# The end of the first expert mixture: three jobs spread by TensorE instead of two, and fetched rows added there

## The chip, the cores and the metric

The kernel runs on one core of a Trainium2 chip. The metric is device time in microseconds, taken as the median of three runs; before the change it is 1932.65 us (1932.41 to 1936.66). All data are 32-bit floats.

## The reference, cut to what matters

The program is two transformer blocks on 256 tokens of width 1024. The change lies in the mixture of experts at the end of the first block: 16 experts of hidden width 256, of which each token takes two.

```python
def hier_moe(h, lp):
    t = h.reshape(B * L, D)                        # 256 x 1024
    ...                                            # group, two experts per token, weights
    combine = jnp.sum(one_hot(e_idx, 16) * w_sel[..., None], axis=1)
    hg = jnp.einsum("nd,edh->neh", t, lp["moe_w_gate"])
    hu = jnp.einsum("nd,edh->neh", t, lp["moe_w_up"])
    a = silu(hg) * hu * combine[..., None]
    return jnp.einsum("neh,ehd->nd", a, lp["moe_w_down"])
...
x = x + mod_l[5] * hier_moe(modulate(rmsnorm(x, norm2_w[l]), mod_l[3], mod_l[4]), lp)
x = rmsnorm(x, norm_f_w)                           # and then the second block
```

## The kernel before, in words

The code calls this mixture `moe1`. It computes each expert only for the tokens that chose it. The 16 experts are taken two at a time, so there are eight **jobs**, numbered 0 to 7. A job has 128 places: 64 for its first expert, 64 for its second.

A job goes through these stages. TensorE gathers its tokens and turns them (`gather`); VectorE and ScalarE each copy one half of that to SBUF (`he_in`). TensorE multiplies by gate and up weights in four parts of one weight cell each (`pair_gate_up`, L1278). ScalarE takes the silu (L1924), VectorE multiplies (L2819) and transposes (L2822), and the semaphore `moe1_actT` tells TensorE. TensorE multiplies by the down weights in two cells (`pair_down`, L1289). VectorE and ScalarE copy the result into a buffer of rows, `pair_ye` (L2829 and L1931), 8 small copies each.

The loop over `s` in `pairs` sets the order on each engine. TensorE does gate and up of job s, with the gather of job s+1 behind the third cell, and then the down product of job s-1; behind the loop the last thing is the down product of job 7. So the down products of jobs 6 and 7 stand in a row.

The rows must get back to the tokens. Jobs 0 to 5 do this through HBM: ScalarE's queue stores the 128 rows of a job (L1937, 0.5 MB), and GpSimd fetches for each token the two rows of its two experts with four indirect DMAs (L679, 0.5 MB each), once these six stores have landed. VectorE weighs the fetched rows (`rows_in`, L2876 and L2879), and adds them to `x` with the block's gate (`add_gated`, L2588 and L2590, once per block of 128 tokens). Jobs 6 and 7 are spread instead: TensorE multiplies their rows by a matrix of weighted ones, `selT2` (the products of L1356: 4 of 128x512 for each job, two per block of tokens), and VectorE adds the sum with `add_gated` too. `SPREAD` says how many jobs are spread. Behind the spread TensorE runs 26 fill products (`busy`, L693), whose results nobody reads.

SyncE issues the loads of the weights into nine cells of 1 MB, in the order in which they are used; a cell is loaded again when TensorE has released it (semaphore `units_used`). The order of everything here is that of the code: no scheduler changes it.

Of the kernel before, what the change touches and what calls it, by code (L numbers as in the profile page):

```python
# [14 lines left out]
P = 128  # L15
T = 256
# [229 lines left out]
SPREAD = {"moe1": 2, "moe2": 1}  # L246
# [104 lines left out]
R_SELT, R_SELW, R_YE2, R_HOT = 512, 2560, 5120, 14464  # L351
# [29 lines left out]
def build(nc, A, blob_in, out):  # L381
    with ExitStack() as ctx:
# [236 lines left out]
        def _(pool):  # L619
# [29 lines left out]
            for i, name in enumerate(("moe1", "moe2")):  # L649
# [4 lines left out]
                with pool.Else():  # L654
# [32 lines left out]
        def _(pe):  # L687
# [545 lines left out]
            def moe_mm(name, i):  # L1233
# [9 lines left out]
                selw, selT2 = region(R_SELW, 2, NT, P), region(R_SELT, 2, T)  # L1243
                pair_actT, pair_ye = region(R_MT, 2, 4, 64), (region(R_YE, D), region(R_YE2, D))
# [63 lines left out]
                def gather(j, x0):  # L1308
# [12 lines left out]
                    if j == jobs - 1 and name == "moe2":  # L1321
                        for b in range(NT):
                            last = nc.tensor.transpose(ps[0:slot_n, x0 + 2, b * P:(b + 1) * P], sel[:, b, :], ident)
                    elif j == jobs - 1:
                        for i_ in range(2):
                            for b in range(NT):
                                last = nc.tensor.transpose(ps[:, j % 2, i_ * T + b * P:i_ * T + (b + 1) * P], selw[:, i_, b, :], ident)
                    last.then_inc(sem(f"{name}_gathered"), 1)

                def pairs():  # L1330

                    gather(0, 2)
# [18 lines left out]
                    for i_ in range(2):  # L1351
                        pe.wait_ge(sem("moe1_ye"), jobs - 1 + i_)
                        pe.wait_ge(sem("moe1_ye_dve"), jobs - 1 + i_)
                        for p in range(4):
                            b, half = divmod(p, 2)
                            last = mm(ps[:, p, :], selT2[:, i_, b * P:(b + 1) * P], pair_ye[i_][:, half * 512:(half + 1) * 512],  # L1356
                                      start=i_ == 0, stop=i_ == 1)
                            if i_:
                                last.then_inc(sem("moe1_spread"), 1)
                    busy(26, 4)  # L1360
# [350 lines left out]
        def _(act):  # L1711
# [184 lines left out]
            def moe_silu(name, i):  # L1896
# [7 lines left out]
                pair_sg, pair_ye = region(R_MG, 4, 64), (region(R_YE, D), region(R_YE2, D))  # L1904
# [9 lines left out]
                def pairs():  # L1914

                    he_in(0, 2)
                    for s in range(jobs + 1):
# [7 lines left out]
                        if s:  # L1925
                            j = s - 1
                            act.wait_ge(used, dn[j][-1][3])
                            if j >= 2:
                                act.wait_ge(sem(f"moe1_stored_{j % 2}"), 16 * (j // 2))
                            for t_, q in ((t_, q) for t_ in range(4) for q in (2, 3)):  # L1930
                                last = ac(pair_ye[j % 2][32 * t_:32 * t_ + 32, q * 256:(q + 1) * 256],  # L1931
                                          ps[32 * q:32 * q + 32, 4 + 2 * (j % 2) + t_ // 2, (t_ % 2) * 256:(t_ % 2 + 1) * 256], ACT.Copy)
                            last.then_inc(sem("moe1_ye"), 1)
                            if j < jobs - SPREAD[name]:
                                act.wait_ge(sem("moe1_ye"), j + 1)
                                act.wait_ge(sem("moe1_ye_dve"), j + 1)
                                act.dma_start(rows_of[name][j * slot_n:(j + 1) * slot_n, :], pair_ye[j % 2]).then_inc(sem(f"moe1_stored_{j % 2}"), 16)  # L1937
# [199 lines left out]
        def _(dve):  # L2137
# [562 lines left out]
            def moe_act(name, i, between):  # L2700
# [14 lines left out]
                selw, selT2 = region(R_SELW, 2, NT, 2, 64), region(R_SELT, 2 * T)  # L2715
# [4 lines left out]
                pair_sg, pair_act, pair_actT, pair_ye = region(R_MG, 4, 64), region(R_MA, 4, 64), region(R_MT, 2, T), (ye, region(R_YE2, D))  # L2720
# [9 lines left out]
                def select_weighted():  # L2730
                    for j in range(2):
                        for b in range(NT):
                            for e in range(2):
                                c = 2 * (jobs - 2 + j) + e
# [8 lines left out]
                def he_in(j, x0):  # L2743
# [5 lines left out]
                    if j == jobs - 1:  # L2749
                        if name == "moe1":  # L2750
                            v.tensor_copy(selT2, ps[:, j % 2, :])
                        else:
                            v.tensor_copy(selT, ps[0:slot_n, x0 + 2, 0:T])
# [55 lines left out]
                def pairs():  # L2809
# [4 lines left out]
                    for s in range(jobs + 1):  # L2814
                        if s < jobs:
                            if s + 1 < jobs:
                                he_in(s + 1, 2)
                            dve.wait_ge(sem("moe1_silu"), s + 1)
# [4 lines left out]
                        if s:  # L2823
                            j = s - 1
                            dve.wait_ge(used, down_[j][-1][3])
                            if j >= 2:
                                dve.wait_ge(sem(f"moe1_stored_{j % 2}"), 16 * (j // 2))
                            for t_, q in ((t_, q) for t_ in range(4) for q in (0, 1)):
                                last = v.tensor_copy(pair_ye[j % 2][32 * t_:32 * t_ + 32, q * 256:(q + 1) * 256],  # L2829
                                                     ps[32 * q:32 * q + 32, 4 + 2 * (j % 2) + t_ // 2, (t_ % 2) * 256:(t_ % 2 + 1) * 256])  # L2830
# [41 lines left out]
                def rows_in():  # L2872

                    dve.wait_ge(sem(f"{name}_rows"), 16 * NT * 2)
# [5 lines left out]
                    fence()  # L2880
                    for b in range(NT):
                        add_gated(b, 0, D, ya[:, b, :], 1)
# [356 lines left out]
```

## Time and profile before

| | |
|---|---|
| time, median of three runs | 1932.65 us |
| profiled execution, its own time | 1931.84 us |
| its span in the trace | 1930.0 us |
| mean granted TensorE clock | 0.991 |
| TensorE (PE) busy | 1832.1 us, 95% |
| VectorE (DVE) busy | 686.6 us, 36% |
| ScalarE (ACT) busy | 312.8 us, 16% |
| first mixture, from its first gate product to the last spread product | 505.6 to 643.7 us |

A time in a row is counted from the start of the span. A 32-bit matmul stands as two rows in the trace, each with a weight load (PEld) of its own; a transposition stands as one. Idle time ahead of an instruction stands in brackets with what ended it; "issue" means that nothing the profile shows was waited for. PEclk is the granted TensorE clock as a share of 2.4 GHz, so 0.50 is 1.2 GHz.

### The profile page before, as it was taken

The numbers are of one execution on the slowest core, as the hardware profiler recorded it, in microseconds if no ns is written. First come the engines' busy times: TensorE is split into PE (matmuls) and PEld (weight loads), VectorE is DVE, ScalarE is ACT, GpSimd is POOL, SyncE is SP. The second block draws the span as 40 slices with busy tenths as digits, with TensorE's granted clock in tenths as the row PEclk, the third lists the DMA queues.
The fourth block names the chain that finished last, engine by engine and source line by source line (L and its number), as shares of the span: only waits on it lengthen the run. The fifth ranks groups of instructions, "written<-read, shape, count | busy, mean of one in ns | idle before, by whom it ended". The sixth has DMA issues, their size and how long they took to land.

```text
span 1930.0 us, 38840 instructions
## 1 busy us (share of the span) xinstructions
PE 1832.1 (95%) x17312; PEld 1069.2 (55%) x17312; DVE 686.6 (36%) x1656; ACT 312.8 (16%) x729; POOL 35.3 (2%) x54
## 2 busy tenths in 40 slices
PE   5999989999887899999999999999999999999997
PEld 2655767885766555577676555443444444343443
DVE  3757782532333665432323553211110111111014
ACT  3221121001233324200001242100000010000001
POOL 0100000000100000000000000000000000000000
PEclk9999999999999999999999999999999999999999
DMA  9968743274799442467675332799999999999995
GB/s 356 370 221 305 262 172 115 85 264 163 281 405 419 162 160 103 151 236 256 229 250 181 131 101 112 288 399 420 409 420 410 415 411 406 419 413 415 408 416 214
DMA packets 157471, 547.75 MB, mean 284 GB/s; under 512 B 10224, under 2 KB 35152, under 8 KB 123072
## 3 DMA queue, kind: packets, MB, share of 16 engines
q1 hardware_dynamic: 149360, 509.15, 68.3%
q0 software_dynamic: 5152, 26.49, 3.9%
q10 hardware_dynamic: 2784, 9.53, 1.3%
q8 instruction: 140, 2.29, 0.5%
q14 instruction: 35, 0.29, 0.0%
HBM read 533.99 MB, written 18.48 MB: 286 GB/s over the span
## 4 chain that ended last, share of the span: by engine, by line
PE 86%; DVE 6%; DMA 2%; issue 2%; DVEq 1%; ACT 1%; SPq 0%; ACTq 0%
PE ps L1266 24%; PE ps L1302 12%; PE ps L1215 8%; PE ps L1499 8%; PE ps L1079 4%; PE ps L1197 4%; PE ps L1227 4%; PE ps L882 4%; PE ps L1278 3%; PE ps L1094 2%; PE ps L1289 1%; DMA ring<-in_ada_w 1%; PE ps L749 1%; PE ps L698 1%; PE ps L1549 1%
## 5 line engine op out<-in xcount | busy, mean ns | idle before, releaser
L1266 PE MATMUL ps<-ring,arena 128*32 128x512 f32 (+1 forms) x4608 | 459.1, 557 | 0.0
L1266 PEld LDWEIGHTS ps<-ring,arena 128*32 128x32 f32 x4608 | 148.9, 110 | 293.9 <-issue 289.5
L1302 PE MATMUL ps<-ring,arena 128*32 128x256 f32 x4224 | 232.1, 379 | 0.0
L1302 PEld LDWEIGHTS ps<-ring,arena 128*32 128x32 f32 x4224 | 137.3, 110 | 98.7 <-issue 12.1
L2851 DVE TENSOR_TENSOR arena<-arena,ps 128x256 f32<-128x256 f32 (+1 forms) x72 | 26.9, 373 | 390.9 <-ACT arena L1952 390.9
L1499 PE MATMUL ps<-ring,hT 128*128 128x512 f32 (+1 forms) x384 | 154.9, 554 | 1.4 <-DVE hT L2201 1.4
L1215 PE MATMUL ps<-hT,ring 128*128 128x256 f32 x704 | 153.8, 379 | 0.7 <-DVE hT L2201 0.7
L1215 PEld LDWEIGHTS ps<-hT,ring 128*128 128x128 f32 x704 | 133.6, 190 | 23.4 <-issue 4.8
L1499 PEld LDWEIGHTS ps<-ring,hT 128*128 128x128 f32 x384 | 69.1, 190 | 68.8 <-issue 66.9
L1079 PE MATMUL ps<-hT,ring 128*128 128x256 f32 x384 | 86.6, 385 | 3.9 <-DMA ring<-in_w_branch 3.9
L1952 ACT ACTIVATE arena<-ps 128x256 f32<-128x256 f32 (+1 forms) x72 | 21.2, 367 | 422.7 <-PE ps L1266 422.7
L1278 PE MATMUL ps<-ring,arena 128*32 128x128 f32 x2048 | 67.2, 285 | 22.8 <-issue 22.5
L882 PE MATMUL ps<-hT,ring 128*128 128x256 f32 x384 | 88.1, 383 | 0.8 <-DVE hT L2201 0.8
L2747 DVE TENSOR_SCALAR arena<-ps,ga,mod 128x128 f32<-128x128 f32 (+1 forms) x64 | 20.8, 388 | 188.8 <-PE ps L1317 140.9
L1079 PEld LDWEIGHTS ps<-hT,ring 128*128 128x128 f32 x384 | 73.8, 193 | 14.5 <-DMA ring<-in_w_branch 4.3
L882 PEld LDWEIGHTS ps<-hT,ring 128*128 128x128 f32 x384 | 71.4, 190 | 17.5 <-issue 6.6
L1227 PE MATMUL ps<-ring,arena 128*128 128x512 f32 x176 | 78.4, 596 | 0.0
L1278 PEld LDWEIGHTS ps<-ring,arena 128*32 128x32 f32 x2048 | 60.2, 115 | 28.8 <-issue 26.7
L2171 DVE SCALAR_TENSOR_TENSOR arena<-ring,cact,arena 128x512 f32<-128x512 f32 x84 | 63.1, 751 | 6.6 <-issue 0.4
L2279 DVE SCALAR_TENSOR_TENSOR grow<-arena,colv,grow 128x189 f32<-128x189 f32 (+2 forms) x160 | 62.1, 429 | 6.3 <-issue 0.4
L2697 DVE TENSOR_TENSOR arena<-arena,ps 128x256 f32<-128x256 f32 x22 | 9.3, 422 | 146.9 <-ACT arena L1894 146.9
L1910 ACT ACTIVATE arena<-ps,mod,ga 128x128 f32<-128x128 f32 (+1 forms) x64 | 23.2, 443 | 218.9 <-PE ps L1317 155.4
(426 smaller groups left out, 1784.9 us busy)
## 6 DMA issues: line engine op xcount, KB each, us to landing
ring<-in_gate_up SPq DMA_DIRECT2D x160, 1024.0 KB, 14.1
ring<-in_down SPq DMA_DIRECT2D x104, 1024.0 KB, 15.5
ring<-in_gate_up_last SPq DMA_DIRECT2D x64, 768.0 KB, 13.4
ring<-in_w_ada SPq DMA_DIRECT2D x48, 768.0 KB, 6.1
ring<-in_w_in SPq DMA_DIRECT2D x36, 768.0 KB, 7.3
ring<-in_ada_w SPq DMA_DIRECT2D x24, 768.0 KB, 10.4
ring<-in_w_ada SPq DMA_DIRECT2D x24, 512.0 KB, 7.1
ring<-in_w_in SPq DMA_DIRECT2D x12, 1024.0 KB, 7.5
```

Source lines behind the costliest of these rows:

```text
L882: last = mm(ps[:, half, (i % 2) * T:(i % 2 + 1) * T], quads[:, s, k * 512 + i * P:k * 512 + (i + 1) * P], src[:, k, :], start=k == 0, stop ...
L1079: last = mm(ps[:, 2 * (n % 2), i * T:(i + 1) * T], w512(s, k, m * P, P), hT[:, k, :], start=k == 0, stop=k == KD - 1)
L1094: last = mm(ps[:, 2 * (n % 2) + 1, i * T:(i + 1) * T], ring[:, s, o:o + P], z[:, y0 + c, :], start=c == 0, stop=c == NBR - 1)
L1197: last = mm(ps[:, 2 * b + half, :], src[:, k, b * P:(b + 1) * P], w512(slots_[half], k), start=k == 0, stop=k == KD - 1)
L1215: m_ = mm(ps[:, hb, i * cols:(i + 1) * cols], ring[:, s, o:o + P], src[:, k, :], start=k == 0, stop=k == KD - 1)
L1227: m_ = mm(ps[:, base + 2 * b + half, :], region(R_AT, 2, T)[:, hb, b * P:(b + 1) * P], ring[:, s, o:o + 512], start=first and hb == 0, sto ...
L1266: last = mm(ps[32 * q:32 * q + 32, base + t_, 0:2 * n], src[:, k, 32 * t_:32 * t_ + 32], w[:, q], start=k == 0, stop=k == KD - 1)
L1278: last = mm(ps[32 * q:32 * q + 32, bank, t_ * P:(t_ + 1) * P], src[:, k, 32 * t_:32 * t_ + 32], w[:, t_ // 2, q], start=k == 0 and t_ == 0 ...
L1302: last = mm(ps[32 * q:32 * q + 32, bank + t_ // 2, (t_ % 2) * 256:(t_ % 2 + 1) * 256], rows[:, t_, o:o + 32], cells[:, cell, r * D + q * 2 ...
L1499: last = mm(ps[:, b, 0:w], hT[:, k, b * P:(b + 1) * P], w512(entry[0], k, 0, w, w), start=k == 0, stop=k == KD - 1)
L2171: last = v.scalar_tensor_tensor(acc, w, cact[:, c + k:c + k + 1], acc, ALU.mult, ALU.add)
L2279: v.scalar_tensor_tensor(acc[:, a, ro, co], grids[a][:, ri, ci], tap(b, (dr + 1) * 3 + dc + 1), acc[:, a, ro, co], ALU.mult, ALU.add)
```

## The change

Job 5 is spread by TensorE too, so that five jobs and not six are stored and fetched. Three of job 5's four spread products stand inside the gate and up products of job 7, behind the third cell (`g == 2`). The rest stands behind the last down product. The weighted rows that were fetched are added in the same sums, by a product with the identity for each of the four banks, and VectorE then adds each block once. The weighing itself (`weigh_rows`) moves on VectorE from behind the last copies to the place ahead of job 7's silu product. The rows of job 7 get a third buffer. The selection matrix of job 5 is made and turned in addition. The fills go from 26 to 18.

```diff
-SPREAD = {"moe1": 2, "moe2": 1}
+SPREAD = {"moe1": 3, "moe2": 1}
+YE_OF = (0, 1, 0, 1, 0, 1, 0, 2)
...
                         for i_ in range(2):
-                            pool.wait_ge(sem(f"moe1_stored_{i_}"), 16 * (stored // 2))
+                            pool.wait_ge(sem(f"moe1_stored_{i_}"), 16 * ((stored + 1 - i_) // 2))
...
-                    elif j == jobs - 1:
-                        for i_ in range(2):
+                    elif name == "moe1" and j >= jobs - 2:
+                        for n, i_ in enumerate((0,) if j == jobs - 2 else (1, 2)):
                             for b in range(NT):
-                                last = nc.tensor.transpose(ps[:, j % 2, i_ * T + b * P:i_ * T + (b + 1) * P], selw[:, i_, b, :], ident)
+                                last = nc.tensor.transpose(ps[:, j % 2, n * T + b * P:n * T + (b + 1) * P], selw[:, i_, b, :], ident)
...
+                TO_BANK = (2, 3, 0, 1)
+                def copied(j):
+                    pe.wait_ge(sem("moe1_ye"), j + 1)
+                    pe.wait_ge(sem("moe1_ye_dve"), j + 1)
+                def spread_job(j, parts):
+                    i_ = j - (jobs - 3)
+                    for p in parts:
+                        b, half = divmod(p, 2)
+                        last = mm(ps[:, TO_BANK[p], :], selT2[:, i_, b * P:(b + 1) * P], pair_ye[YE_OF[j]][:, half * 512:(half + 1) * 512],
+                                  start=i_ == 0, stop=i_ == 2)
+                        if i_ == 2:
+                            last.then_inc(sem("moe1_spread"), 1)
...
                                 pair_gate_up(g, gu[s][g], he[:, s % 2], s % 2)
+                                if g == 2 and s == jobs - 1:
+                                    pe.wait_ge(sem("moe1_actT"), s)
+                                    copied(jobs - 3)
+                                    spread_job(jobs - 3, (0, 1, 2))
...
-                    for i_ in range(2):
-                        pe.wait_ge(sem("moe1_ye"), jobs - 1 + i_)
-                        pe.wait_ge(sem("moe1_ye_dve"), jobs - 1 + i_)
-                        for p in range(4):
-                            ...
-                    busy(26, 4)
+                    copied(jobs - 2)
+                    spread_job(jobs - 2, (0, 1, 2))
+                    spread_job(jobs - 3, (3,))
+                    spread_job(jobs - 2, (3,))
+                    for p in range(4):
+                        b, half = divmod(p, 2)
+                        mm(ps[:, TO_BANK[p], :], ident, rows_sum[:, b, half * 512:(half + 1) * 512], start=False, stop=False)
+                    copied(jobs - 1)
+                    spread_job(jobs - 1, range(4))
+                    busy(18, 4)
...
-                            if j >= 2:
+                            if 2 <= j < jobs - 1:
                                 act.wait_ge(sem(f"moe1_stored_{j % 2}"), 16 * (j // 2))
...
                 def select_weighted():
-                    for j in range(2):
+                    for j in range(3):
...
                             if s + 1 < jobs:
                                 he_in(s + 1, 2)
+                            if s == jobs - 1:
+                                weigh_rows()
                             dve.wait_ge(sem("moe1_silu"), s + 1)
...
-                    rows_in()
                     for b in range(NT):
                         dve.wait_ge(sem("moe1_spread"), 2 * b + 2)
-                        add_gated(b, 0, D, all_ps[:, b * D:(b + 1) * D], 1).then_inc(sem("block_in"), 1)
+                        add_gated(b, 0, D, all_ps[:, (1 - b) * D:(2 - b) * D], 1).then_inc(sem("block_in"), 1)
```

The new lines have other numbers: L1278 becomes L1280, L1289 becomes L1291, L1356 becomes L1344, L2876 becomes L2908, L2588 becomes L2611. On TensorE, from the third gate and up cell of job 7 on, there stood:

```order
L1278 MATMUL ps<-ring,arena 32x128 [waits cell3_full]
L1278 MATMUL ps<-ring,arena 32x128 x31
L1278 MATMUL ps<-ring,arena 32x128 [waits cell4_full]
L1278 MATMUL ps<-ring,arena 32x128 x31
...
L1289 MATMUL ps<-ring,arena 32x256 x15
L1356 MATMUL ps<-arena 128x512 [waits moe1_ye_dve,moe1_ye]
L1356 MATMUL ps<-arena 128x512 x3
L1356 MATMUL ps<-arena 128x512 [waits moe1_ye_dve,moe1_ye]
L1356 MATMUL ps<-arena 128x512 x3
L693 MATMUL ps<-blob 128x256 x26
```

and now there stands:

```order
L1280 MATMUL ps<-ring,arena 32x128 [waits cell3_full]
L1280 MATMUL ps<-ring,arena 32x128 x31
L1344 MATMUL ps<-arena 128x512 [waits moe1_ye_dve,moe1_ye,moe1_actT]
L1344 MATMUL ps<-arena 128x512 x2
L1280 MATMUL ps<-ring,arena 32x128 [waits cell4_full]
L1280 MATMUL ps<-ring,arena 32x128 x31
...
L1291 MATMUL ps<-ring,arena 32x256 x15
L1344 MATMUL ps<-arena 128x512 [waits moe1_ye_dve,moe1_ye]
L1344 MATMUL ps<-arena 128x512 x4
L1380 MATMUL ps<-arena,blob 128x512 x4
L1344 MATMUL ps<-arena 128x512 [waits moe1_ye_dve,moe1_ye]
L1344 MATMUL ps<-arena 128x512 x3
L694 MATMUL ps<-blob 128x256 x18
```

Three spread products are now ahead of the fourth cell, five and four identity products (L1380) ahead of the four of job 7. On VectorE, from the copies of job 5 on, there stood:

```order
L2829 COPY arena<-ps 32x256 x7
L2819 TENSOR_TENSOR arena<-arena,ps 128x256 [waits moe1_silu]
L2822 STREAM_TRANSPOSE arena<-arena 128x256
L2829 COPY arena<-ps 32x256 [waits moe1_stored_0,units_used]
L2829 COPY arena<-ps 32x256 x7
L2829 COPY arena<-ps 32x256 [waits moe1_stored_1,units_used]
L2829 COPY arena<-ps 32x256 x7
L2876 TENSOR_SCALAR arena<-arena 128x1024 [waits moe1_rows]
L2876 TENSOR_SCALAR arena<-arena 128x1024
L2879 SCALAR_TENSOR_TENSOR arena<-arena 128x1024 x2
L2588 TENSOR_TENSOR xn<-arena,grow 128x1024
L2590 TENSOR_TENSOR x<-x,xn 128x1024
```

and now there stands:

```order
L2855 COPY arena<-ps 32x256 x7
L2908 TENSOR_SCALAR arena<-arena 128x1024 [waits moe1_rows]
L2908 TENSOR_SCALAR arena<-arena 128x1024
L2911 SCALAR_TENSOR_TENSOR arena<-arena 128x1024 x2
L2845 TENSOR_TENSOR arena<-arena,ps 128x256 [waits moe1_silu]
L2848 STREAM_TRANSPOSE arena<-arena 128x256
L2855 COPY arena<-ps 32x256 [waits moe1_stored_0,units_used]
L2855 COPY arena<-ps 32x256 x7
L2855 COPY arena<-ps 32x256 [waits units_used]
L2855 COPY arena<-ps 32x256 x7
L2611 TENSOR_TENSOR xn<-ps,grow 128x1024 [waits moe1_spread]
L2613 TENSOR_TENSOR x<-x,xn 128x1024
```

The weighing with its wait for the fetched rows (`moe1_rows`) has moved ahead of job 7's silu product, and the two pairs of L2588 and L2590 that read `arena` are gone.

## Rows read from the trace of the kernel before

**Rows 1.** Timeline of TensorE, jobs 6 and 7: start, length, instructions, idle before.

```profile
613.16 0.42 PE L1278 MATMUL ps<-ring,arena 128*32 128x128 f32 x6 [0.96 <-issue]
613.39 3.66 PE L1289 MATMUL ps<-ring,arena 128*32 128x256 f32 x64
616.84 1.74 PE L1278 MATMUL ps<-ring,arena 128*32 128x128 f32 x56
619.49 3.70 PE L1278 MATMUL ps<-ring,arena 128*32 128x128 f32 x128 [0.90 <-issue]
625.68 3.27 PE L1278 MATMUL ps<-ring,arena 128*32 128x128 f32 x72 [2.50 <-issue]
628.65 7.79 PE L1289 MATMUL ps<-ring,arena 128*32 128x256 f32 x128
```

**Rows 2.** Timeline of all engines, from job 7's silu to the next stage.

```profile
629.41 0.42 DVE L2819 TENSOR_TENSOR arena<-arena,ps 128x256 f32<-128x256 f32 x1 [8.87 <-ACT arena L1924]
...
629.92 0.45 DVE L2822 STREAM_TRANSPOSE arena<-arena 128x256 f32<-128x256 f32 x1
...
633.04 6.88 DVE L2829 COPY arena<-ps 32x256 f32<-32x256 f32 x16 [2.67 <-PE ps L1289]
...
636.61 7.13 PE L1356 MATMUL ps<-arena 128*128 128x512 f32 x16 [0.18 <-DVE arena L2829]
...
639.95 1.42 DVE L2876 TENSOR_SCALAR arena<-arena 128x1024 f32<-128x1024 f32 x2
...
643.57 11.39 PE L693 MATMUL ps<-blob 128*128 128x256 f32 x52
...
644.00 1.23 DVE L2588 TENSOR_TENSOR xn<-arena,grow 128x1024 f32<-128x1024 f32 x1
...
649.39 1.23 DVE L2588 TENSOR_TENSOR xn<-ps,grow 128x1024 f32<-128x1024 f32 x1
...
661.15 3.40 PE L815 MATMUL ps<-blob,xn 128*128 128x128 f32 x16 [6.19 <-DVE xn L2975]
```

**Rows 3.** Stretches: length, busy PE, PEld, DVE, ACT, POOL; PEclk, DMA share, GB/s.

```profile
612.80:620.00 7.20, 5.94 (x146) 4.74 (x150) 3.67 (x9) 3.19 (x9) 0.00 (x0) 1.00 1.02 421
620.00:627.00 7.00, 4.50 (x160) 4.29 (x153) 0.53 (x2) 0.21 (x1) 0.00 (x0) 0.97 1.01 416
627.00:630.00 3.00, 3.00 (x53) 2.53 (x46) 0.50 (x2) 0.38 (x1) 0.13 (x1) 0.50 0.54 223
...
661.00:664.00 3.00, 2.85 (x13) 2.69 (x14) 1.68 (x4) 0.00 (x0) 0.00 (x0) 0.50 0.00 0
```

**Rows 4.** DMA queues from 604 to 622 us: packets, MB, share.

```profile
q8 instruction: 3, 0.05, 1.1%
```

**Rows 5.** Stores of jobs 4 and 5, and the first gather.

```profile
603.60 0.33 ACTq L1937 DMA_DIRECT2D rows_moe<-arena  x1
...
620.62 0.33 ACTq L1937 DMA_DIRECT2D rows_moe<-arena  x1
...
629.87 0.98 POOL L679 DMA_INDIRECT arena<-rows_moe,rowi  x1 [49.36 <-DMA rows_moe<-arena]
```

**Rows 6.** The same gathers in the second mixture: first issue, and who waits for them.

```profile
1859.30 1.01 POOL L679 DMA_INDIRECT arena<-rows_moe,rowi  x1 [225.70 <-DMA rows_moe<-arena]
...
1879.49 1.41 DVE L2876 TENSOR_SCALAR arena<-arena 128x1024 f32<-128x1024 f32 x2 [8.00 <-DMA arena<-rows_moe,rowi]
```

**Rows 7.** DMA queues from 1859.3 to 1879.4 us.

```profile
q1 hardware_dynamic: 1007, 6.21, 74.6%
q0 software_dynamic: 576, 2.10, 26.2%
```

**Rows 8.** DMA queue of the weights from 612.8 to 633 us; last cell, issued 615.38.

```profile
q1 hardware_dynamic: 843, 6.06, 72.0%
...
ring<-in_down SPq DMA_DIRECT2D x1, 1024.0 KB, 16.0
```

**Rows 9.** TensorE's first long stall, while the sorted rows are written.

```profile
523.80 2.61 PE L1278 MATMUL ps<-ring,arena 128*32 128x128 f32 x49 [3.22 <-issue]
```

More of the change, by code:

```diff
@@ L1927, in pairs @@
                             act.wait_ge(used, dn[j][-1][3])
-                            if j >= 2:
+                            if 2 <= j < jobs - 1:
                                 act.wait_ge(sem(f"moe1_stored_{j % 2}"), 16 * (j // 2))
                             for t_, q in ((t_, q) for t_ in range(4) for q in (2, 3)):
-                                last = ac(pair_ye[j % 2][32 * t_:32 * t_ + 32, q * 256:(q + 1) * 256],
+                                last = ac(pair_ye[YE_OF[j]][32 * t_:32 * t_ + 32, q * 256:(q + 1) * 256],
                                           ps[32 * q:32 * q + 32, 4 + 2 * (j % 2) + t_ // 2, (t_ % 2) * 256:(t_ % 2 + 1) * 256], ACT.Copy)
@@ L2730, in select_weighted @@
                 def select_weighted():
-                    for j in range(2):
+                    for j in range(3):
                         for b in range(NT):
                             for e in range(2):
-                                c = 2 * (jobs - 2 + j) + e
+                                c = 2 * (jobs - 3 + j) + e
                                 v.tensor_scalar(selw[:, j, b, e, :], iota[:, 0:cap], slots[:, b, c:c + 1], comb[:, b, c:c + 1],
@@ L2748, in he_in @@
                                         ga[:, 8 + k:9 + k], mod[:, 24 + k:25 + k], ALU.mult, ALU.add)
[L2749 to L2753, printed above, removed]
+                    if name == "moe1" and j >= jobs - 2:
+                        lo, hi = (0, T) if j == jobs - 2 else (T, 3 * T)
+                        v.tensor_copy(selT2[:, lo:hi], ps[:, j % 2, 0:hi - lo])
+                    elif j == jobs - 1:
+                        v.tensor_copy(selT, ps[0:slot_n, x0 + 2, 0:T])
                     fence()
@@ L2825, in pairs @@
                             dve.wait_ge(used, down_[j][-1][3])
-                            if j >= 2:
+                            if 2 <= j < jobs - 1:
                                 dve.wait_ge(sem(f"moe1_stored_{j % 2}"), 16 * (j // 2))
                             for t_, q in ((t_, q) for t_ in range(4) for q in (0, 1)):
-                                last = v.tensor_copy(pair_ye[j % 2][32 * t_:32 * t_ + 32, q * 256:(q + 1) * 256],
+                                last = v.tensor_copy(pair_ye[YE_OF[j]][32 * t_:32 * t_ + 32, q * 256:(q + 1) * 256],
                                                      ps[32 * q:32 * q + 32, 4 + 2 * (j % 2) + t_ // 2, (t_ % 2) * 256:(t_ % 2 + 1) * 256])
                             last.then_inc(sem("moe1_ye_dve"), 1)
-                    rows_in()
                     for b in range(NT):
                         dve.wait_ge(sem("moe1_spread"), 2 * b + 2)
-                        add_gated(b, 0, D, all_ps[:, b * D:(b + 1) * D], 1).then_inc(sem("block_in"), 1)
+                        add_gated(b, 0, D, all_ps[:, (1 - b) * D:(2 - b) * D], 1).then_inc(sem("block_in"), 1)
                         between(b)
@@ L2872, in rows_in, with weigh_rows @@
                 def rows_in():
+                    weigh_rows()
+                    for b in range(NT):
+                        add_gated(b, 0, D, ya[:, b, :], 1)
+                    fence()
+                def weigh_rows():
                     dve.wait_ge(sem(f"{name}_rows"), 16 * NT * 2)
@@ L2879, in rows_in @@
                         v.scalar_tensor_tensor(ya[:, b, :], yb[:, b, :], roww[:, 2 + b:3 + b], ya[:, b, :], ALU.mult, ALU.add)
-                    fence()
-                    for b in range(NT):
-                        add_gated(b, 0, D, ya[:, b, :], 1)
                     fence()
```

21 lines of the change are left out of this document (9 added, 12 removed).

## The prediction

> **What bounds the kernel now.** I read the page first. TensorE is busy 95% of the span, so any change that moves TensorE's next stage moves the end. Then I took the timeline from 600 to 665 us, because the changed code ends there and the next stage (L815, then the next block's weights) starts at 661.15 [rows 2]. Going back from that start, the work is a row on VectorE without a gap that matters: add the spread sums and norm (from 649.39), before that add the fetched rows (from 644.00), before that weigh them (from 639.95), before that copy jobs 6 and 7 (6.88 us from 633.04) [rows 2]. Those copies follow TensorE's last 128 rows of down products, which end at 628.65 + 7.79 = 636.44 [rows 1]. So the stage is bound by TensorE to 636.44 and by VectorE from there to 661. What has to be predicted is one number: when VectorE starts its first pair L2588/L2590 on the spread sums, 649.39 now. What follows that start is the same work in both kernels.
>
> Two things about TensorE before 636.44 matter. It stalls: 0.96, 0.90 and 2.50 us of "issue" [rows 1]. Between stalls it runs 6 + 64 + 56 = 126 rows and then 128 rows, with their weight loads 256 instructions, and a run starts every 6.2 us (613.16, 619.49, 625.68). Job 7 has had 56 + 128 = 184 rows (185 at most) when the 2.50 us stall comes, while a cell is 64 rows, so that the stall stands 7 rows before the end of the third cell: it isn't a wait for a cell's weights. The instruction queue moved three packets of 16 KB in the 18 us from 604 to 622 [rows 4], one per 6 us. I read these stalls as the next 256 instructions arriving late, while the DMA engines are full (share 1.02 and 1.01, 421 and 416 GB/s, [rows 3]). Second, after the 2.50 us stall the granted clock falls to 0.50 (1.2 GHz) until 630 [rows 3]: 0.03 of 7 us and half of 3 us, so 1.7 us of work lost. The check: 72 rows at 0.027 and 128 rows at 0.054 (3.45 us for 64, [rows 1]) are 8.9 us; 625.68 + 8.9 + 1.7 = 636.3, and the trace has 636.44.
>
> The Trainium skill (page "Runtime: NRT & Kernel Launch", section "Instruction fetch mechanics") says that instructions come in blocks of 16 KB, 256 instructions, and that crossing a block's edge is mostly hidden. The size agrees with the 128 rows; the hiding doesn't hold here, by the 2.50 us. Taken by its word, the stall would be another wait, at the cell; that is rival C below.
>
> **The change part by part.**
>
> *Three spread products of job 5 ahead of the fourth cell.* They need job 5's copies, which are done before its store at 620.62 [rows 5], so they don't wait. A spread product is two rows; 16 rows take 7.13 us [rows 2], so 0.43 each and 2.57 us for three. Would they fill the 2.50 us hole? The hole is at an edge of 256 instructions. The new code has two more transpositions ahead of it (job 5's selection), so the edge comes after 182 to 183 rows of job 7; the spread products stand behind row 192. They come behind the hole: 9 rows later. The hole stays, and the fall of the clock with it, and TensorE gets 2.57 + 0.05 us longer. Down of job 7 would end at 636.44 + 2.62 = 639.06, down of job 6 at 635.6 (3.45 before). Bounds: 0 (all hidden) and 2 x 2.57 (all at 1.2 GHz); I take 2.6, since the slow stretch costs its 1.7 us whatever work lies in it.
>
> *Five stores and not six; gathers early.* Job 4's store is issued at 603.60. Job 5's took 629.87 - 620.62 = 9.25 us until the gathers went out [rows 5], so now they go out at 612.85, not 629.87. There they meet full DMA engines. When do they land? The nearest case is the second mixture's end: same four gathers, same full engines, first issue 1859.30, VectorE let go at 1879.49 [rows 6], 20.2 us; they had 26.2% of the engines against the weights' 74.6% [rows 7]. From 612.85 this is 633.0. The bytes agree: weights still to come after 612.8 are 6.06 MB [rows 8], with 2.10 MB of gathers 8.16 MB, at 0.42 MB/us 19.4 us, so the engines are full until 632.2. Bounds: without company the gathers landed before 639.95, at most 10.1 us after 629.87, which gives 623; with the slow case 633.
>
> *The wait on VectorE.* Behind the weighing, in VectorE's order, stand job 7's product and transposition, on which TensorE's last down product waits, and then job 6's copies. Weighing takes 644.00 - 639.95 = 4.05 us [rows 2]: 633.0 to 637.1. Product and transposition: 629.41 to 630.37, 0.96 us, and 0.1 until TensorE goes on: 638.15. TensorE is ready for it at 635.6, so it now waits 2.5 us. The break-even is a landing at 630.5; each us later costs one.
>
> *The end of TensorE.* Down of job 7: 638.15 + 3.45 = 641.6. Copies on VectorE: job 6 from 638.1 to 641.5, job 7 from 641.7 to 645.1 (3.42 each, half of 6.88). TensorE: from 641.75 five spread and four identity products, 9 x 0.86 = 7.7, to 649.5; job 7's copies are done by then. Two of its four products, 1.7 us, and 0.2 to VectorE: 651.4. Before: 649.39. The identity products (3.4 us) and the spread of job 6 and the rest of job 5 (4.3 us) replace VectorE's 4.05 of weighing and 5.39 of adding (644.00 to 649.39) behind the copies; 9.4 us go and 7.7 + 1.7 + 0.2 less the 3.4 us of job 7's copies come.
>
> *Nothing.* The third buffer for job 7 removes a wait that isn't late. Four more selection products, one more copy and two transpositions lie where the engines wait for DMA. 18 fills instead of 26 end about 652.9 + 7.9 (11.39 us for 26, [rows 2]) = 660.8, ahead of the next stage; TensorE's idle time before it shrinks from 6.19 us [rows 2] to about 2.4, so that the clock of 0.50 at 661 to 664 [rows 3] might not come: up to 0.5 us back, which I don't count. The last weight cell lands 16.0 us after 615.38, at 631.4 [rows 8]; with 2.10 - 0.52 MB more in the engines 3.8 us later, 635.2, and its first use is at 638.15 + 1.7.
>
> **Sum.** 651.4 - 649.39 = +2.0 us. Profiled execution: 1931.84 + 2.0 = 1933.8; the median of the runs is 0.8 above it, so 1934.6. Own range of this case: landing at 632 to 634, 1933.6 to 1935.6, up to 1936.3 if the new wait of 2.5 us drops the clock once more (1.7 us, as after the stall).
>
> **Rivals.** *B, the gathers land early.* If the two queues shared evenly, 2.10 MB at 210 GB/s would take 10 us, landing about 624, and the weighing would be over at 628, before job 7's silu. Then TensorE doesn't wait: 639.06 + 0.1 + 7.7 + 1.7 + 0.2 = 648.8, so -0.6: 1932.1. For it: by 627 the weights thin out in the kernel before (0.54 share, [rows 3]). Against it: 20.2 us and 26% in [rows 6, 7]. The Trainium skill (page "DMA: Bandwidth & Descriptors", section "Queues, rings and completion order") has each engine take turns between its queues packet by packet, which with packets of one size means even shares and this rival; the 26.2% speak against it.
>
> *C, the hole is filled.* If the stall is a wait at the cell, or the edge lies later than I count, three products vanish in it and the clock may stay up. With early gathers: 636.44 + 0.1 + 9.6 = 646.2, -3.2; with the 1.7 us of clock -4.9: 1929.5 to 1927.7. With late gathers VectorE's wait covers it and A's time stands. Against: the count of rows.
>
> *D, the instruction blocks come later still, slower than before.* A third busy queue beside weights and instructions (the gathers, 613 to 633) could stretch 6.2 us per block by half, to 9.3. The blocks that start at 613.16 and 619.49 then hand over 3.1 us later each: TensorE +6.2, the late gathers hidden behind it, 648.8 + 6.2 = 655.0, +5.6, and with a second 1.7 us at 1.2 GHz +7.3: 1938.3 to 1940.0. It decides from a block time of about 7.4 us up, where it passes the wait for the gathers. For it: the longest stall, 3.22 us [rows 9], is in the stretch where sorted rows are written. Against: job 4's store, also a further queue, ran in part beside the block before 613.16, and the cadence stayed.
>
> **Chances.** A 0.50, with a second fall of the clock 0.14 of these; B 0.22; C 0.11; D 0.12; 0.05 for what I don't see. A measurement of this kernel tells no change from one below about 0.3%, 5.8 us: faster is below 1926.9, slower above 1938.4. A, B and nearly all of C lie within. Faster: 0.01 of C and 0.03 unseen, 0.04. Slower: most of D and the rest, 0.10. Same: 0.86. The range from B and the upper part of C to D's lower end: 1929.5 to 1938.5.
>
> **What would show it.** Gathers issued at 612 to 614; VectorE idle before L2908 until 631 to 634, released by DMA; TensorE idle 2 to 3 us before the last 64 rows of L1291; the 2.5 us stall still 7 to 10 rows ahead of the three spread products; first L2611 at 650.5 to 652. Wrong if VectorE doesn't wait at L2908 (B), if the spread products start at 623 (C), or if blocks of 128 rows start over 7 us apart from 613 on (D).

## The result, and the profile after

The changed kernel takes 1939.5 us (median of 14 runs, 1934.87 to 1946.22). The kernel before, run beside it 14 times, takes 1935.18 us (1930.33 to 1937.4) and not the 1932.65 of its first three runs. The ratio is 1.0028, 95% interval 1.0020 to 1.0037: slower by 5.4 us (3.9 to 7.3). I had forecast 1934.6, +2.0, within 1929.5 to 1938.5. The direction of the 2.0 was right. By my bound of 0.3% (5.8 us) this is still no change, if barely; but with this many runs the interval lies wholly on the slow side, and the time lies 1.0 us above the range. Of the 4.9 us missed, 2.5 are the kernel before, since the median of its first three runs lies that much below the median of all 14. The other 2.4 are the change by the medians (4.3 apart for 2.0), or 3.4 by the ratio.

The page after shows the one store of 0.5 MB less (the queue of the stores had 2784 packets and 9.53 MB before). TensorE is busy for 1844.1 us and no longer 1832.1; the other engines are within 4 us of before.

```profile
span 1937.4 us, 38839 instructions
...
q10 hardware_dynamic: 2640, 9.00, 1.2%
...
HBM read 533.99 MB, written 17.96 MB: 285 GB/s over the span
```

TensorE after (start, length, instructions, idle before): a stall at 609 us, and then from the down product of job 5 to the fills. It answers to [rows 1] and the L1356 and L693 of [rows 2].

```profile
609.47 3.58 PE L1280 MATMUL ps<-ring,arena 128*32 128x128 f32 x60 [2.50 <-issue]
...
617.28 3.26 PE L1291 MATMUL ps<-ring,arena 128*32 128x256 f32 x19 [0.33 <-issue]
620.86 2.59 PE L1291 MATMUL ps<-ring,arena 128*32 128x256 f32 x43 [0.33 <-issue]
...
630.39 0.60 PE L1280 MATMUL ps<-ring,arena 128*32 128x128 f32 x10 [1.72 <-issue]
630.92 2.84 PE L1344 MATMUL ps<-arena 128*128 128x512 f32 x6
633.69 1.95 PE L1280 MATMUL ps<-ring,arena 128*32 128x128 f32 x64
635.46 3.64 PE L1291 MATMUL ps<-ring,arena 128*32 128x256 f32 x64
641.70 3.66 PE L1291 MATMUL ps<-ring,arena 128*32 128x256 f32 x64 [2.60 <-DVE arena L2848]
645.29 4.56 PE L1344 MATMUL ps<-arena 128*128 128x512 f32 x10
649.69 3.60 PE L1380 MATMUL ps<-arena,blob 128*128 128x512 f32 x8
653.12 3.60 PE L1344 MATMUL ps<-arena 128*128 128x512 f32 x8
656.55 7.93 PE L694 MATMUL ps<-blob 128*128 128x256 f32 x36
```

The other engines after: job 4's store, the first gather, the weighing, the first sum. They answer to [rows 5] and [rows 2].

```profile
605.98 0.33 ACTq L1960 DMA_DIRECT2D rows_moe<-arena  x1
...
615.22 0.99 POOL L680 DMA_INDIRECT arena<-rows_moe,rowi  x1 [32.99 <-DMA rows_moe<-arena]
...
636.64 1.42 DVE L2908 TENSOR_SCALAR arena<-arena 128x1024 f32<-128x1024 f32 x2 [9.51 <-DMA arena<-rows_moe,rowi]
...
655.04 1.22 DVE L2611 TENSOR_TENSOR xn<-ps,grow 128x1024 f32<-128x1024 f32 x1 [6.19 <-PE ps L1344]
```

These rows show the forecast chain: three spread products 10 rows behind the stall (1.72 us) and not in it, VectorE held 9.51 us by the gathers, TensorE held 2.60 us by VectorE's transposition. From VectorE's release to the first sum are 18.4 us, as forecast (633.0 to 651.4). The gathers take longer: 615.22 to 636.64 is 21.4 us, not 20.2. The DMA queues meanwhile, 615.2 to 636.6 us (packets, MB, share), next to [rows 7]:

```profile
q1 hardware_dynamic: 836, 6.01, 67.6%
q0 software_dynamic: 576, 2.10, 24.6%
```

And the granted clock (last but two) is 1.2 GHz just where the next stage's weight products start, at 670.82; before, it had fallen and come back by then [rows 3]:

```profile
668.00:670.00 2.00, 1.62 (x8) 1.48 (x8) 0.79 (x2) 0.00 (x0) 0.00 (x0) 0.50 0.00 0
670.00:674.00 4.00, 3.67 (x7) 1.60 (x6) 1.57 (x4) 1.94 (x4) 0.00 (x0) 0.50 0.02 4
```

To compare profiles I use three stretches. **S** runs from the issue of job 4's store to VectorE's first sum: 603.60 to 649.39, 45.8 us before; 605.98 to 655.04, 49.1 after. **N** runs from there to the next stage's first weight product (15.8 in both). **T** runs from that product to the last run of 8 rows before 770 us (92.8 before, 94.5 after). These give 3.3 + 0 + 1.7 = 5.0 us. The spans differ by 7.4; 2.4 of it had come ahead of job 4's store, 0.7 of that ahead of the mixture, and differs as much between profiles of one kernel.

### The profile page after: what moved, and what is told of

The parts are those of the page before. It is cut to its first block, busy times and chain, and to the rows that moved or that the text cites. A ratio compares the mean times of both kernels' runs of the same rounds, so it can differ in the third digit from the quotient of the medians.

```text
span 1937.4 us, 38839 instructions
## 1 busy us (share of the span) xinstructions
PE 1844.1 (95%) x17314; PEld 1068.8 (55%) x17314; DVE 682.9 (35%) x1657; ACT 313.1 (16%) x729; POOL 35.3 (2%) x54
## 4 chain that ended last, share of the span: by engine, by line
PE 85%; DVE 6%; DMA 3%; issue 2%; DVEq 1%; ACT 1%; SPq 0%; POOL 0%; ACTq 0%; POOLq 0%
PE ps L1268 23%; PE ps L1304 12%; PE ps L1522 8%; PE ps L1216 8%; PE ps L1080 4%; PE ps L1198 4%; PE ps L1228 4%; PE ps L883 4%; PE ps L1280 3%; PE ps L1095 2%; PE ps L750 1%; DMA ring<-in_ada_w 1%; PE ps L1291 1%; PE ps L699 1%; DMA arena<-rows_moe,rowi 1%
## 5 line engine op out<-in xcount | busy, mean ns | idle before, releaser
L2876 DVE TENSOR_TENSOR arena<-arena,ps 128x256 f32<-128x256 f32 (+1 forms) x72 | 26.9, 373 | 390.6 <-ACT arena L1975 390.6
L1280 PE MATMUL ps<-ring,arena 128*32 128x128 f32 x2048 | 69.5, 283 | 21.1 <-issue 20.6
L1975 ACT ACTIVATE arena<-ps 128x256 f32<-128x256 f32 (+1 forms) x72 | 21.2, 367 | 421.9 <-PE ps L1268 421.9
L1280 PEld LDWEIGHTS ps<-ring,arena 128*32 128x32 f32 x2048 | 61.0, 114 | 28.9 <-issue 27.2
```

The lines of the kernel that those rows point to most:

```text
L1280: last = mm(ps[32 * q:32 * q + 32, bank, t_ * P:(t_ + 1) * P], src[:, k, 32 * t_:32 * t_ + 32], w[:, t_ // 2, q], start=k == 0 and t_ == 0 ...
```

## The experiments

All stretches in us; "gaps" says whether TensorE's rows have the short stops told of in the last section. The ratio is the time against the kernel before, run beside it, with its interval. The changed kernel ran 14 times; of the others, the one with the spread products behind and the one with the weighing first ran 6 times, the rest 12 times. The two kernels that say "again" are one more execution each.

| kernel | fills | S | N | T | gaps | ratio |
|---|---|---|---|---|---|---|
| before | 26 | 45.8 | 15.8 | 92.8 | no | 1 |
| before, again | 26 | 47.5 | 15.8 | 93.8 | yes | |
| changed | 18 | 49.1 | 15.8 | 94.5 | yes | 1.0028 (1.0020 to 1.0037) |
| changed, again | 18 | 51.0 | 15.8 | 92.8 | yes | |
| changed, 23 fills | 23 | 51.3 | 15.3 | 92.8 | yes | 1.0017 (1.0007 to 1.0026) |
| changed, spread products behind | 18 | 52.6 | 15.8 | 94.7 | no | 1.0045 (1.0030 to 1.0061) |
| changed, weighing last | 18 | 45.2 | 15.8 | 92.8 | yes | 0.9997 (0.9984 to 1.0011) |
| the same, 23 fills | 23 | 44.2 | 15.3 | 92.8 | no | 0.9997 (0.9986 to 1.0008) |
| weighing last, gathers held | 18 | 48.0 | 15.3 | 92.8 | yes | 1.0000 (0.9990 to 1.0010) |
| changed, weighing behind job 7's turn | 23 | 51.6 | 15.3 | 92.8 | no | 1.0019 (1.0007 to 1.0032) |
| identity and one sum only | 18 | 42.7 | 15.8 | 94.8 | yes | 0.9983 (0.9972 to 0.9994) |
| the same, 23 fills | 23 | 41.9 | 15.3 | 92.8 | no | 0.9982 (0.9972 to 0.9993) |
| the same, weighing first | 18 | 55.8 | 15.8 | 94.7 | no | 1.0059 (1.0043 to 1.0075) |
| before, four more gathers | 26 | 47.6 | 15.8 | 92.8 | no | 1.0023 (1.0012 to 1.0034) |

**Identity products and one sum, alone.** The kernel before, with:

```diff
+                    for p in range(4):
+                        b, half = divmod(p, 2)
+                        if half == 0:
+                            pe.wait_ge(sem("moe1_ye_dve"), jobs + b + 1)
+                        mm(ps[:, p, :], ident, rows_sum[:, b, half * 512:(half + 1) * 512],
+                           start=False, stop=True).then_inc(sem("moe1_spread"), 1)
-                    busy(26, 4)
+                    busy(18, 4)
...
-                    rows_in()
+                    weigh_rows()
```

> The kernel before (two jobs spread, gathers at the old time), with one part of the change: the weighed rows are added by identity products behind the spread products, VectorE adds once per block, 18 fills. I measure stretch S, from the issue of job 4's store to VectorE's first pair on the spread sums: 45.8 us before, 49.1 after. Theory 1 (the loss is the early gathers, for which VectorE and behind it TensorE wait): S = 45.8 - 3.8 = 42.0, since 5.4 us of adding on VectorE give way to two identity products, 1.7 us; time about 3 us below before. Rival (the identity products and fewer fills are the loss): S at or above 45.8, time not below before. If the clock falls to 1.2 GHz inside the next stage, as it did after the change, up to 1.5 us of the gain are lost there.

S is 42.7 for 42.0, the time 0.9983, 3.3 us below before. This part of the change is a gain. T is 94.8: the clock took 2.0 us of the gain in the profile.

**Weighing last.** The changed kernel, with the weighing behind the last copies and the identity products behind job 7's spread products:

```diff
-                            if s == jobs - 1:
-                                weigh_rows()
...
+                    weigh_rows()
```

> The changed kernel with the weighing taken back behind job 7's copies (and the identity products behind job 7's spread products, waiting for it); gathers still early, three jobs spread. Theory 1 (VectorE's wait ahead of job 7's product): TensorE's 2.6 us wait before its last 64 down rows goes, S = 46.1 against 49.1 after. Rival 2 (gathers that run while the DMA engines are full slow TensorE's own issue, the 0.33 us gaps from 617 to 621): the gaps stay and cost 3 us, so S falls no further than 46.1 and would be 43 without them. Rival 3 (the wait was harmless, other work sets the end): S stays at 49.

Its TensorE, last down products and spread:

```profile
630.99 7.09 PE L1291 MATMUL ps<-ring,arena 128*32 128x256 f32 x128
638.27 7.96 PE L1344 MATMUL ps<-arena 128*128 128x512 f32 x18 [0.19 <-DVE arena L2854]
```

No wait between the two down products; S is 45.2 (forecast 46.1) and the loss in time is gone, though the gathers are still early. Rival 3 fell. Rival 2 can't be told from the 0.9 us by which S lies below 46.1. What speaks against it is that the loss went while the gaps stayed, and that two kernels below have a long S (52.6 and 51.6) without any gaps.

**Gathers held until job 7's product.** The same, with one wait more on GpSimd:

```diff
+                        pool.wait_ge(sem("moe1_act"), MOE_JOBS[name])
```

> As the kernel with the weighing last, and the gathers are held until VectorE has made job 7's product, about where they went out before the change. Theory 1: the early gathers cost by VectorE's wait alone, so S is the same as with the weighing last, within 0.5 us (46.1). Rival 2 (the gathers slow TensorE's issue and instruction blocks): S is 2.5 to 3 us lower than with the weighing last, 43 to 43.5, and no 0.33 us gaps in TensorE's down rows of job 5.

Both were off: S is 48.0. The wait let the gathers go only at 639.20, and TensorE's last down products then had gaps and took 9.6 us for 7.1:

```profile
637.31 5.86 PE L1292 MATMUL ps<-ring,arena 128*32 128x256 f32 x94
643.50 1.12 PE L1292 MATMUL ps<-ring,arena 128*32 128x256 f32 x5 [0.33 <-issue]
644.97 1.95 PE L1292 MATMUL ps<-ring,arena 128*32 128x256 f32 x29 [0.35 <-issue]
```

The gaps stand at the gathers' new place, and holding the gathers gains nothing (1.0000 against 0.9997). So this run doesn't separate the cost of full DMA engines from that of the gaps.

**23 fills.** The changed kernel with `busy(23, 4)`.

> The changed kernel with 23 fill products instead of 18, so that TensorE's idle time before the next stage falls from 2.3 us to about 0.1. Theory 3 (part of the loss is the clock, which after the change fell to 1.2 GHz at 668 to 674 us, inside the next stage's first weight products, where before it fell at 657 to 664 us, while TensorE was idle): clock 1.00 from 666 to 674, the next stage 1.5 us shorter, time 1.5 us below the changed kernel. Rival: the clock's fall comes anyway, or it costs nothing on the whole: same time as the changed kernel within 0.5 us.

N is 15.3 and T 92.8, as the clock theory has it. By the ratios the time is 2.1 us below the changed kernel's (1.5 forecast), but the intervals overlap, so this is not shown. In the profile S was longer: TensorE waited 4.75 us, and in that wait the clock fell, so that the last 64 down rows took 5.18 us and not 3.66. TensorE, and the clock from 646 to 648:

```profile
646.32 5.18 PE L1291 MATMUL ps<-ring,arena 128*32 128x256 f32 x64 [4.75 <-DVE arena L2848]
```

```profile
646.00:648.00 2.00, 1.68 (x16) 0.78 (x20) 1.95 (x6) 0.00 (x0) 0.00 (x0) 0.51 0.02 4
```

**The three spread products behind.** The lines `if g == 2 and s == jobs - 1` with their `spread_job` go, and job 5 is spread in one piece behind the last down product.

> The changed kernel with the three spread products of job 5 taken out of job 7's gate products and put behind the last down product. Theory 1 (TensorE waits for VectorE, which waits for the gathers, so those 2.6 us are hidden): job 7's down product starts no earlier, the wait before it grows by 2.6 us, and the end is 2.6 us later: S about 2.5 us above the changed kernel's 49.1 and 51.3, time 1.5 to 3 us above it. Rival (the three products in the gate stage are what made the change slower): S falls by 2.6 us instead, the time too.

S is 52.6, 1.3 to 3.5 above the changed kernel's three profiles, and the time 3.3 us above it (1.0045 to 1.0028; the intervals overlap). The wait grew to 5.42 us. From VectorE's release by the gathers (635.96) to the first sum (658.28) are 22.3 us, of which 1.4 are a fall of the clock: 2.6 us more than the changed kernel's 18.4, which is what the three products take. So they were hidden in the wait before. The run also shows that job 6's down weights now come late:

```profile
633.67 1.93 PE L1291 MATMUL ps<-ring,arena 128*32 128x256 f32 x32 [1.73 <-DMA ring<-in_down]
641.02 5.00 PE L1291 MATMUL ps<-ring,arena 128*32 128x256 f32 x64 [5.42 <-DVE arena L2843]
```

**Identity and one sum, 23 fills.**

> The kernel with only the identity products and one sum, with 23 fills instead of 18. Clock theory: no idle time of 2.3 us before the next stage, clock 1.00 through its transpositions and first weight products, so the stretch from the first sum to the first weight product is 15.3 us and not 15.8, and from there to the last one of the stage 87.6 and not 89.7: up to 2.5 us below the kernel with 18 fills in its profile, about 1 to 2.5 in the time, and 4 to 6 us below the kernel before. Rival (the fall of the clock doesn't matter on the whole): same time as with 18 fills.

N and T came as forecast, S 41.9. The time didn't follow: 0.9982 against 0.9983, far inside the intervals, so the clock's share in the mean is below what this can tell. The next stage of the kernel with 23 fills begins at full clock (before: [rows 2], 3.40 us for both transpositions):

```profile
656.05 1.09 PE L815 MATMUL ps<-blob,xn 128*128 128x128 f32 x8 [0.15 <-DVE xn L2986]
657.78 1.09 PE L815 MATMUL ps<-blob,xn 128*128 128x128 f32 x8 [0.63 <-DVE xn L2986]
659.61 17.41 PE L1504 MATMUL ps<-ring,hT 128*128 128x512 f32 x40 [0.74 <-DVE hT L2206]
```

This is the kernel to keep: it and its sister with 18 fills are the only ones whose whole interval lies below before.

**Four more gathers in the middle.** The kernel before; behind the fetch of job 5:

```diff
+                        if name == "moe1" and j == 5:
+                            for t_ in range(2):
+                                for b in range(NT):
+                                    pool.indirect_dma_start(region((R_YA, R_YB)[t_], NT, D)[:, b, :], None, sorted_of[name][:, :],
+                                                            bass.IndirectOffsetOnAxis(ap=rowj[:, 2 * t_ + b:2 * t_ + b + 1], axis=0)
+                                                            ).then_inc(sem(f"{name}_rows"), 16)
```

> The kernel before, with four more indirect gathers (2.1 MB, of the sorted rows, into the same SBUF rows that the real ones fill later) issued right behind the fetch of job 5, about 547 us, in the middle of the stage; nobody waits for them but the real gathers. It measures by itself what gathers cost beside TensorE's small products and full DMA engines. Theory 1: weights come 2.1 MB / 0.42 = 5.0 us later in the end if the DMA engines bound the stage, and 0 to 1 us if TensorE's own instruction blocks do; time +1 or below. Rival 2 (GpSimd's indirect DMAs slow TensorE's issue): gaps of about 0.33 us in TensorE's rows for 4 to 5 us from 1 us behind the first issue, 2.5 to 3 us lost there, of which the stalls between blocks give back a part: +1 to +3 us.

The time rises by 4.4 us (2.3 to 6.6). The gaps of rival 2 aren't there, but this profile has none at its other gathers and at its scatter either (last section), so it doesn't test that rival. Theory 1 had named the way, later weights, but had put it at 1 us or below. From 587 to 607 us TensorE waits for seven weight cells, 5.6 us in all, and from 623 us for five more; the kernel before waits for none there. Three of these waits:

```profile
587.31 1.95 PE L1286 MATMUL ps<-ring,arena 128*32 128x128 f32 x64 [1.57 <-DMA ring<-in_gate_up]
589.80 1.96 PE L1286 MATMUL ps<-ring,arena 128*32 128x128 f32 x64 [0.54 <-DMA ring<-in_gate_up]
...
596.02 1.93 PE L1297 MATMUL ps<-ring,arena 128*32 128x256 f32 x32 [0.74 <-DMA ring<-in_down]
```

So this stage has almost no DMA time to spare: 2.1 MB are 5.0 us at 0.42 MB/us, and 4.4 of them show.

**Weighing last, 23 fills.**

> The changed kernel with the weighing last (three jobs spread, gathers early) and 23 fills. If only VectorE's wait and the clock made the change slow, this is below the kernel before: S 45.2 as with 18 fills, 15.3 us to the next stage's first weight product and 87.6 us to its last, time 1 to 3 us below before. Against the kernel with two jobs spread and 23 fills it tells what spreading a third job is worth: by S (45.2 against 42.7) it is worth less than nothing, 2.5 us.

S is 44.2, and the time as before (0.9997) where 1 to 3 us below was forecast. The third job spread gains nothing here: against two jobs spread with the same fills S is 2.3 us longer and the time 2.9 us (0.9997 to 0.9982; the intervals overlap). With 18 fills the two kernels lie the same way, 2.5 us apart in S and 2.7 in time.

**Weighing first, rows late.** Identity and one sum only, with `weigh_rows()` moved ahead of job 7's silu product.

> The kernel with only the identity products and one sum (two jobs spread, gathers at the old time, S = 42.7), but with the weighing ahead of job 7's silu product as in the change. The fetched rows land 36.1 us after job 4's store here and not 31. Theory 1 (VectorE holds job 7's product back until the rows land, and TensorE's last down product with it, one us for one): weighing over at 40.2, last down product from 41.2 to 44.7, copies of job 7 to 48.2, spread and identity products to 53.4, S = 53.6, and up to 55.1 if the clock falls in the wait of more than 5 us: 11 to 12.4 us above 42.7, and the time about 10 us above that kernel. Rival (the place of the weighing doesn't matter, TensorE has other work): S within 1 us of 42.7.

The wait, on VectorE and on TensorE:

```profile
638.18 1.42 DVE L2880 TENSOR_SCALAR arena<-arena 128x1024 f32<-128x1024 f32 x2 [18.89 <-DMA arena<-rows_moe,rowi]
```

```profile
643.24 5.30 PE L1290 MATMUL ps<-ring,arena 128*32 128x256 f32 x64 [12.06 <-DVE arena L2827]
```

S is 55.8 for 53.6 to 55.1, 13.1 above the kernel it was made from, the time 14.7 us above it (about 10 forecast). The place of the weighing alone does this, with the fall of the clock that its wait brings.

**Weighing behind job 7's turn.** The changed kernel with 23 fills, `weigh_rows()` two instructions later.

> The changed kernel with 23 fills and the weighing moved by two instructions, behind job 7's product and transposition. Theory 1: TensorE's last down product no longer waits (2.6 and 4.75 us in the two profiles so far), but job 6's copies do, until the weighing is over 35 us after job 4's store: S about 48.2, against 49.1 and 51.3, and 45.2 and 44.2 with the weighing last; so the time is 1 to 3 us below the changed kernel with 23 fills and still above the kernel before. Rival (only the wait of the down product counts): S as with the weighing last, 44 to 45.

S is 51.6, not 48.2. The wait moved from TensorE's down product to its first spread product, and the clock fell there instead (10 rows in 7.44 us, 4.56 in the changed kernel):

```profile
641.89 7.44 PE L1344 MATMUL ps<-arena 128*128 128x512 f32 x10 [3.44 <-DVE arena L2855]
```

With the 2.9 us of clock taken out it is 48.7. The time isn't better either: 1.0019, against 1.0017 with the weighing ahead of job 7's product. Job 6's copies stand behind the weighing here, and TensorE needs them as soon as its down product is done. The last job's down weights came late as well, by 0.69 and 0.43 us.

**Both kernels once more.** No edit; a second profile of each.

> The kernel before, once more, for a second profile: how far the stretches vary by themselves. Theory 1 takes S = 45.8 as the mark of this kernel: within 1 us of it, 15.8 us to the next stage's first weight product and 92.8 us on to the last product of its first part. Rival (the differences of 3 to 5 us in S between the kernels are chance): S beyond 47.

> The changed kernel, once more. Theory 1: S between 49 and 52, rows landing 21.2 to 21.4 us after the first gather is issued, TensorE's wait before the last down product 2.5 to 5 us; if it is above 3.4 us, the clock falls and that product takes 5 us and not 3.7. Clock theory: after the 18 fills the clock falls either in the transpositions (next part 92.8 us) or inside the weight products (94.5 to 94.8 us). Rival (chance): S within 1 us of the kernel before.

The kernel before has S 47.5, beyond the bound from which I had said that the differences may be chance, and T 93.8. The changed kernel has S 51.0, a wait of 5.25 us and a last down product of 4.99 us. The two executions took 1936.1 and 1943.8 us. The changed kernel's TensorE and VectorE, this time:

```profile
613.00 1.94 PE L1280 MATMUL ps<-ring,arena 128*32 128x128 f32 x60 [2.49 <-issue]
...
640.77 1.42 DVE L2908 TENSOR_SCALAR arena<-arena 128x1024 f32<-128x1024 f32 x2 [11.76 <-DMA arena<-rows_moe,rowi]
...
645.83 4.99 PE L1291 MATMUL ps<-ring,arena 128*32 128x256 f32 x64 [5.25 <-DVE arena L2848]
```

So S of one kernel varies by 2 us, and differences below that from single profiles say nothing. The kernels are 3.8 us apart in the mean (46.6 from two profiles and, over the three with the changed S, 50.4) and don't overlap.

## Why the prediction was wrong, point by point

The mechanism was right; the sum failed in the sizes of its terms. The forecast of +2.0 is an S of 47.8 us (603.60 to 651.4). The three profiles with the changed S (49.1, 51.0, 51.3) are that number and three terms, within 0.1 us: the gathers go out later (0.0, 0.8, 0.8), they take longer (1.3, 1.1, 1.2), and the clock falls in TensorE's wait (0, 1.4, 1.5). To this comes the clock in the next stage, which the sum had at nothing. The points:

*What bounds the end: right.* The start of the first sum carries over; N is the same 15.8.

*The hole isn't filled: right.* The three products stand 10 rows behind the stall in every profile of the changed kernel. Rival C fell. But the fall of the clock that I had left behind this stall came in none of the three.

*The gathers: mechanism right, size short.* In the changed kernel's profiles they went out 9.2, 10.0 and 10.0 us after the store (9.25 forecast) and landed 21.2 to 21.4 us later (20.2 forecast from [rows 6]). Each of these us costs one. Rival B fell, and with it the even shares: 24.6% of the engines.

*VectorE's wait: mechanism right, and it is the cause.* Weighing last takes the loss away; weighing first with later rows makes it 14.7 us. TensorE waits 2.60, 4.75 and 5.25 us for a forecast of 2.5. That the first fits is partly luck: the rows landed late, and TensorE was late by nearly as much. There the clock had fallen behind the stall at 609.47, so that 60 rows took 3.58 us, where they took 1.94 us in the other two.

*The clock in that wait: the term that I under-priced.* I gave a second fall 14% and 1.7 us. It came in two of the three, for 1.4 and 1.5 us. Over all kernels it didn't come after the wait of 2.60 us, and came in each of the five profiles with a wait of 3.44 us or more in that place, for 1.3 to 2.9 us. This doesn't make 2.60 us a safe length: behind the stalls of 2.50 us the clock fell in some profiles and not in others.

*"Nothing" for the fills: wrong in sign.* I had 18 fills give up to 0.5 us back. In profiles with 18 fills and about 2.3 us idle, T was 1.7 to 2.0 us longer in four of seven. With 23 fills N was 0.5 shorter and T undisturbed in all four. By the mean that is about 1.1 us for 18 fills, and 0.35 in the three profiles with 26, so about 0.8 us lost where I had up to 0.5 gained. The runs' times don't show it: 23 fills and 18 can't be told apart in any of the three pairs. The Trainium skill (page "TensorE: Matmul & The Clock Gate", section "What's actually happening") says that the default state is throttled, that activity releases it, and that the instant of the release at a kernel's start differs from run to run. The trace agrees that it differs, in the middle of the kernel too: the changed kernel's clock is low inside the next stage's weight products in one of its profiles with 18 fills, and back at 1.00 before them in the other.

*"Nothing" for the DMA: right here, but with little to spare.* Early gathers make weights late: 1.73 us at job 6's down product when TensorE arrives early, and 4.4 us of the time with 2.1 MB more in the middle. In the changed kernel's three profiles TensorE waits for no weights.

*Sum.* S +3.8 and the clock +0.8 give +4.6, the ratio says +5.4 (3.9 to 7.3); the 0.8 left isn't settled. Against +2.0, 1.8 in S were missing: 1.7 for the gathers and 1.0 for the clock in the wait, less the 0.9 by which the kernel before has a longer S over two profiles than in its first. Another 0.8 was missing in the next stage's clock. And the range was drawn from three runs of the kernel before: 2.5 us higher, on its 14 runs, it would have held 1939.5. Rival D, the blocks stretched by half, didn't come: blocks started 6.1 to 7.2 us apart in the changed kernel's profiles, not 9.3. Its time of 1938.3 to 1940.0 holds the measured one by chance.

## What to carry to other kernels

Moving work "to where the engine is idle" moves its wait too. What matters is what stands behind the waiting instruction in that engine's order: here a 1 us job on which another engine's last product hung. Two instructions further back the wait cost as much, because the next work behind it was needed too. A wait should be last in the order of its engine, unless the data is sure to be there. And a wait of TensorE costs more than its length when the clock falls in it.

## What the runs showed of the hardware that I had not expected

In 7 of the 14 profiles TensorE's rows stop every 0.7 us for about 0.3 us, for some 4 us, from about 1 us after GpSimd's first indirect DMA. In the other 7 they run smoothly at the same place. A profile that has the gaps at the scatter of job 0 also has them at the gathers, and the kernel before has them in one of its two profiles: so it is something of the execution, not of the kernel. In the changed kernel's profile, TensorE and GpSimd:

```profile
510.53 0.43 PE L1280 MATMUL ps<-ring,arena 128*32 128x128 f32 x4 [0.29 <-issue]
511.13 0.95 POOL L660 DMA_INDIRECT sorted_moe<-xn,rowj  x1 [0.30 <-issue]
511.24 0.43 PE L1280 MATMUL ps<-ring,arena 128*32 128x128 f32 x4 [0.28 <-issue]
...
511.97 0.45 PE L1280 MATMUL ps<-ring,arena 128*32 128x128 f32 x6 [0.30 <-issue]
```

From the first gate product to job 4's store it costs about 2 us in the mean: 97.3 to 99.8 us with gaps, 96.0 to 98.0 without (the kernel with four more gathers left out). What slows TensorE's issue there wasn't found. It can be only a part of the spread of the runs of one kernel, 5 to 13 us here.
